# A two-layer hybrid trunk on one core: scale loads, cast order, a table load and layer norm sums rearranged

## What is computed

```python
shift, scale, gate = jnp.split((cond @ w_ada[layer] + b_ada[layer])[:, None, :], 3, axis=-1)
h = rms_norm(x, norm_g[layer]) * (1.0 + scale) + shift
...
u = causal_depthwise_conv(a_half * jax.nn.sigmoid(b_half), conv_b_w[layer]) + conv_b_b[layer]
y_b = jax.nn.silu(layer_norm(u, ln_b_g[layer], ln_b_b[layer])) * jax.nn.silu(z_b)
...
merged = (g_a * (y_a @ w_proj_a[layer]) + g_b * (y_b @ w_proj_b[layer])
          + g_c * (y_c @ w_proj_c[layer]))
x = x + gate * (merged @ w_out[layer])
```

## Time and profile before

| | |
|---|---|
| median of 3 runs | 2340.78 us (2339.74 to 2343.28) |
| the profiled execution's own time | 2340.51 us |
| its span, first to last instruction | 2338.7 us |
| PE / PEld (weight loads) busy | 2255.2 us (96%) / 2040.3 us (87%) |
| POOL busy | 1646.5 us (70%) |
| DVE busy | 1141.1 us (49%) |
| ACT busy | 955.9 us (41%) |
| mean granted TensorE clock | 0.977 of full |
| moved by DMA | 479.65 MB, mean 205 GB/s |

### The profile page before, as it was taken

One profiled execution on the slowest core, in us unless ns is written; L12 is line 12 of the kernel. 1 busy time (PEld: TensorE's weight loads), 2 busy tenths in 40 slices (PEclk: granted clock), 3 DMA queues, 4 the chain that ended last, 5 costly groups with the idle time before them and its releaser, 6 DMA issues.

```text
span 2338.7 us, 40293 instructions
## 1 busy us (share of the span) xinstructions
PE 2255.2 (96%) x16408; PEld 2040.3 (87%) x16408; DVE 1141.1 (49%) x1682; ACT 955.9 (41%) x1037; POOL 1646.5 (70%) x676
## 2 busy tenths in 40 slices
PE   5799999999999999999899999999999999999999
PEld 3789999987779988888899999998777899888899
DVE  5849883854443443443522894665544335421110
ACT  3234444472322544434234344437433244444442
POOL 1468778765554788987666886876655458888876
PEclk8789999999999999999999999999999999999999
DMA  9967545544442589897865664554444337976664
GB/s 370 386 210 225 164 142 177 161 148 124 129 137 92 200 310 332 296 329 284 323 208 181 195 213 142 168 166 145 138 134 134 113 118 279 343 233 190 204 207 154
DMA packets 228840, 479.65 MB, mean 205 GB/s; under 512 B 22080, under 2 KB 26304, under 8 KB 220128
## 3 DMA queue, kind: packets, MB, share of 16 engines
q1 hardware_dynamic: 227392, 475.50, 61.1%
q10 hardware_dynamic: 1312, 2.23, 0.3%
HBM read 471.25 MB, written 6.29 MB: 204 GB/s over the span
## 4 chain that ended last, share of the span: by engine, by line
POOL 48%; issue 35%; PE 16%; POOLq 1%; DVE 0%; ACT 0%; DVEq 0%; ACTq 0%
POOL wl L519 48%; PE ps L908 5%; PE ps L910 5%; PE ps L909 5%; POOLq L518 1%; PE ps L1331 0%; PE ps L997 0%; POOLq L514 0%; DVE xs L1985 0%; DVE ps L1709 0%; ACT gate L528 0%; POOLq L519 0%; DVEq L1367 0%; ACTq L770 0%; DVEq L1708 0%
## 5 line engine op out<-in xcount | busy, mean ns | idle before, releaser
L519 POOL TENSOR_TENSOR wl<-raw,wh 128x1024 fp32r<-128x1024 f32 x672 | 1646.3, 2460 | 679.2 <-ACT wh L540 677.8
L540 ACT CAST wh<-raw 128x1024 fp32r<-128x1024 f32 x672 | 702.8, 1049 | 1227.4 <-PE ps L910 1069.0
L908 PE MATMUL ps<-ah,wh 128*128 128x256 f32 x3008 | 873.8, 290 | 40.8 <-DVE al L1477 21.6
L909 PE MATMUL ps<-al,wh 128*128 128x256 f32 x3008 | 861.0, 286 | 0.0
L910 PE MATMUL ps<-ah,wl 128*128 128x256 f32 x3008 | 860.5, 286 | 0.0
L908 PEld LDWEIGHTS ps<-ah,wh 128*128 128x128 f32 x3008 | 588.0, 195 | 48.1 <-DVE al L1477 21.9
L909 PEld LDWEIGHTS ps<-al,wh 128*128 128x128 f32 x3008 | 587.8, 195 | 4.5 <-issue 4.1
L910 PEld LDWEIGHTS ps<-ah,wl 128*128 128x128 f32 x3008 | 587.4, 195 | 0.0
L908 PE MATMUL ps<-wh,ah 128*128 128x512 f32 (+1 forms) x832 | 325.7, 391 | 0.0
L910 PE MATMUL ps<-wh,al 128*128 128x512 f32 (+1 forms) x832 | 318.7, 383 | 0.0
L909 PE MATMUL ps<-wl,ah 128*128 128x512 f32 (+1 forms) x832 | 318.5, 383 | 0.0
(11 more groups left out here) (259 smaller groups left out, 1810.9 us busy)
## 6 DMA issues: line engine op xcount, KB each, us to landing
raw<-w_in SPq DMA_DIRECT2D x512, 512.0 KB, 3.5
modw<-w_ada SPq DMA_DIRECT2D x64, 1024.0 KB, 7.6
adaw<-w_ada SPq DMA_DIRECT2D x64, 512.0 KB, 9.6
raw<-w_out SPq DMA_DIRECT2D x64, 512.0 KB, 5.0
raw<-w_pc SPq DMA_DIRECT2D x32, 512.0 KB, 3.6
raw<-w_pb SPq DMA_DIRECT2D x32, 512.0 KB, 5.7
raw<-w_pa SPq DMA_DIRECT2D x32, 512.0 KB, 4.9
gbias<-b_gate SPq DMA_DIRECT2D x24, 256.0 KB, 4.3
```

Of the source, the lines that this page charges most:

```text
L519: nc.gpsimd.tensor_tensor(wl[:, s], raw[:, s], wh[:, s].bitcast(F32), ALU.subtract).then_inc(sem("w_split"), 1)
L540: A.copy(wh[:, s], raw[:, s]).then_inc(sem("w_rounded"), 1)
L908: M.matmul(o, lh, rh, start=start, stop=False, skip_group_check=True)
L909: M.matmul(o, lh, rr, start=False, stop=False, skip_group_check=True)
```

## The change

- **Scale loads.** Units 4 to 15 were loaded and used four per output group; now the first group has units 4 and 5, the second 6 to 10, the third 11 to 15. The load of unit 4 comes one round later in SP's list, that of 5 two later, and so on by `SCALE_AT`. Unit 2 of scale moves on DVE ahead of the three `merged_low`, and adds into `acc` instead of PSUM (UNIT_S is 3); unit 3 stays behind the last merge.
- **Casts.** ACT casts five rounds, not two, before it waits for `yb_ready` and copies to `yh`; three follow.
- **Root's table.** An activation Sqrt of one column is put before the squares of the last group of layer 0. Its result goes to `craw`, which nothing reads.
- **Layer norm sums.** DVE first adds the 8 tiles of `ub`, and later of `lnt`, with one `tensor_reduce` each into the new `lss` (128 x 256 each); PE sums over partitions with one matmul each, not eight. The first reduce lies in the third turn of branch c, after the second step of the inverse; the second between `scan_v(2)` and `z_silu(2)`.

```diff
-        UNIT_A, UNIT_W, UNIT_S = 4, 4, 2
+        UNIT_A, UNIT_S = 4, 3
+        UNIT_W = (UNIT_A, 6, 11, KT)
...
-        SCALE_AT = {(0, 3): 4, (0, 5): 5, (0, 6): 6, (0, 7): 7, (1, 1): 8, (1, 3): 9, (1, 5): 10, (1, 7): 11,
-                    (2, 1): 12, (2, 3): 13, (2, 5): 14, (2, 7): 15}
+        SCALE_AT = {(0, 4): 4, (0, 7): 5, (1, 1): 6, (1, 3): 7, (1, 4): 8, (1, 6): 9, (1, 7): 10,
+                    (2, 1): 11, (2, 3): 12, (2, 4): 13, (2, 6): 14, (2, 7): 15}
...
-                rounds(hc + 8, 2)
+                rounds(hc + 8, 5)
                 act.wait_ge(sem("yb_ready"), L1)
                 act.wait_ge(sem("w_used"), proj_end)
                 A.copy(yh[:], ub[:]).then_inc(sem("yh_ready"), 1)
-                rounds(hc + 10, 6, 2)
+                rounds(hc + 13, 3, 1)
...
                     rounds(hc, 3)
+                    A.activation(craw[:, 0:1], epsb[:, 0:1], ACT.Sqrt)
                     for half in range(2):
                         act.wait_ge(sem("x_half"), half + 1)
...
-                    for kt in range(CT):
-                        mm = M.matmul(pb[3][:, 0:T], ones, ub[:, kt], start=kt == 0, stop=kt == CT - 1)
-                    mm.then_inc(sem("ln_sum"), 1)
+                    pe.wait_ge(sem("ln_tiles"), L1)
+                    M.matmul(pb[3][:, 0:T], ones, lss[:, 0], start=True, stop=True).then_inc(sem("ln_sum"), 1)
...
-                    for kt in range(CT):
-                        mm = M.matmul(pb[3][:, T:2 * T], ones, lnt[:, kt], start=kt == 0, stop=kt == CT - 1)
-                    mm.then_inc(sem("ln_var"), 1)
+                    M.matmul(pb[3][:, T:2 * T], ones, lss[:, 1], start=True, stop=True).then_inc(sem("ln_var"), 1)
...
+                def ln_tiles(n):
+
+                    if n == 0:
+                        V.tensor_reduce(lss[:, 0], ub[:].rearrange("p c t -> p t c"), AX.X, ALU.add
+                                        ).then_inc(sem("ln_tiles"), 1)
...
-                    prep_turn(i, split_yc if i == 0 else None)
+                    prep_turn(i, split_yc if i == 0 else ln_tiles if i == 2 else None)
...
-                V.tensor_tensor(lnt[:, 4:8], ub[:, 4:8], ub[:, 4:8], ALU.mult).then_inc(sem("ln_sq"), 1)
+                V.tensor_tensor(lnt[:, 4:8], ub[:, 4:8], ub[:, 4:8], ALU.mult)
                 scan_v(2)
+                V.drain()
+                V.tensor_reduce(lss[:, 1], lnt[:].rearrange("p c t -> p t c"), AX.X, ALU.add
+                                ).then_inc(sem("ln_sq"), 1)
                 z_silu(2, 0, zs[1])
...
+                units(2, 3)
                 for q in range(3):
                     merged_low(q)
                 merge(3, hc, 12 * layer + 8, False)
-                units(2, 4)
+                units(3, 4)
...
-                            for kt in range(UNIT_A + UNIT_W * j, UNIT_A + UNIT_W * (j + 1)):
+                            for kt in range(UNIT_W[j], UNIT_W[j + 1]):
```

More of the change, by code:

```diff
@@ L241, in trunk @@
         lnt = sb("lnt", 122, [CT, T])
+        lss = sb("lss", 172, [2, T])
         xs = sb("xs", 130, [KT, T])
```

## The result

| | before | after |
|---|---|---|
| median | 2340.26 us (2338.14 to 2343.28, 4 runs) | 2315.37 us (2313.75 to 2318.0, 4 runs) |
| ratio | | 0.9894, 95% interval 0.9879 to 0.9909 |
| profiled execution, span | 2340.51, 2338.7 us | 2315.05, 2313.3 us |
| mean granted clock | 0.977 | 0.982 |

The change gains 24.9 us (1.06%); 30.6 us were forecast, 5.7 us too much. The range of 2305 to 2318 us held the time, and the sign was right. A second set of runs gave 2316.99 us and a ratio of 0.9894 (0.9876 to 0.9912).

The account below looks back on a forecast made before the run. PE, busy in 96% of the span, was taken as the bound. Casts 10.2, sums 11.4, scale loads 8.1 and table 0.9 us made 30.6 us, so 2340.8 - 30.6 = 2310.2 us, range 2305 to 2318.

Parts of the forecast that it names:

- I take the whole excess: Second za group, both layers: five casts ahead remove all time lost at PE's two stops, 6.2 + 4.0 = 10.2 us.
- The part of the bound that named POOL as late behind the later cast: Casts' lower bound, second za group: 5 us gained if POOL is still late by half of each stop.
- PE without idle at the second za group: Expected sign in the changed profile: no PE idle there in both layers, with casts of five rounds ahead.
- I left one eighth of 3.27 us: Layer norm sums: seven of eight matmuls go, 2.86 of 3.27 us, twice per layer, 11.4 us in all.
- The rule of the Trainium skill's page "SBUF — State Buffer": Rival for the new reduces: strided reads make them slow; at 9.1 us each, 15.4 us lost, 2326 us, chance 0.06.
- My cover of 4.2 us: First reduce, between two steps of the inverse: PE is held only from about 4.2 us on, one for one.
- I had said 1138 us: Output stage: SP stands before unit 8 until about 1138 us, when DVE has done unit 6.
- late by about 1 us, and single rounds behind a unit by up to 2.6 us: Rounds of the second and third output groups wait on DMA; 2 us given back, bounds 0 and 8.
- DMA becomes the bound: Rival for output groups two and three: three rounds 2.6 us late each, 6 us given back, 2316 us, chance 0.2.
- some 2 us of the range: Lower end of the range: one less stretch at 1.2 GHz somewhere, some 2 us faster.

Follow-up runs that it names:

- the doubled reduce: The changed kernel with the first reduce over tiles done twice, its result used once; measured once, 2328.62 us.
- the other placing: The changed kernel with DVE doing three, five and four scale units in the first three output groups, loads moved to match; 2316.25 us, ratio to before 0.9883.

## Why the prediction was right, and where it was off

The change did what the mechanism said at each of its places, and the time lies inside the range; the forecast was 5.7 us too high. By term:

- **Casts.** Forecast 10.2 us, measured 10.1 at the stops, net 7.7 us. The step that failed is "I take the whole excess": it gave every split 2.46 us, while those of rounds 208 and 211 took 4.4 us in both layers, each beside a DVE instruction with two SBUF inputs. The part of the bound that named POOL as late behind the later cast had the right victim; PE idles 0.24 to 0.66 us there, and a round costs up to 0.95 us more. The sign "PE without idle at the second za group" was wrong by that.
- **Sums.** Forecast 11.4 us, measured 12.1: I left one eighth of 3.27 us, 0.41, and what stays takes 0.25.
- **The reduce.** I took 2.29 us and the price is 3.83 to 3.88, 1.7 times the adjacent one. The rule of the Trainium skill's page "SBUF — State Buffer", section "Specifications (TRN2)", that I had set as a rival (each access that crosses to a new 16-byte line pays a penalty) agrees in direction. But the two reduces differ in their outputs as well, 256 sums of 8 elements against 8 of 256, and no run separates the two. The size lay inside the cover. My cover of 4.2 us was confirmed by the doubled reduce (3.18 us held, 3.3 worked out), so the time was right although the price was not. With 0.4 us to spare that is partly luck.
- **Scale loads.** Forecast 10.1 gone and 2 back. Measured 9.9 gone and 3.55 back. The stop is as foretold: SP stands until DVE has done unit 6, and that came at 1125.46 us. I had said 1138 us on the clock of the kernel before; the casts and sums of layer 0 had taken 12.1 us from all times by then (6.0 and 2 x 3.03), which makes 1125.9. The term "late by about 1 us, and single rounds behind a unit by up to 2.6 us" was sized at 2 us and is 3.55, in five rounds. The DMA share from 1133 to 1176 us is 0.93 at 350 GB/s, less than the 397 of the earlier trace rows; but it is 1.03 from 1140 to 1150 us, where PE waits longest. That the stop for unit 8 is the cause is not shown: the other placing has no such stop and gives 3.16 us back, but it has a stand of 8.1 us before unit 5. The rival "DMA becomes the bound", which I gave 0.2, is the other part of this; at 6 us it was priced too high. Which part is how large stays open.
- **Table.** Forecast 0.9, measured 0.8 (PE idle 6.26 to 5.30 us, a step of 0.55 alone). Alone it cannot be told from no change.
- **What the sum lacked.** The clock appeared only as a gain behind stops that went, and as some 2 us of the range. The trace of before had a half-clock stretch behind three of the four one-column blocks, and I had not looked at what PE did ahead of each.

Together: 30.6 forecast less 2.4 (POOL), 1.5 (scale loads), 0.3 (scale and casts at the stops), 0.1 (table), plus 0.7 (sums) is 27.0; the remaining 2 us to the measured 24.9 are, by the profiles, clock and single waits, and lie within what one kernel's runs differ by.

## What to carry to other kernels

Before moving work beside a co-running engine, list which of its instructions share a port with the neighbour, and price the neighbour's instruction as theirs plus its own: a split of 2.4 us took 4.4. A cover is worth working out even for an operation whose price is unknown, since it told here at which price the time would change. Test a supposed cause by an edit that brings no second one: the other placing of the loads took one stop of SP away and made another, and so could not tell the stop from DMA's rate. And on a kernel that keeps TensorE busy, read the granted clock behind every block of tiny matmuls: spreading 64 of them gained 7 us, nearly a third of what the whole change gained, and took no work away.

## What the runs showed of the hardware

- A DVE `tensor_reduce` of 2048 elements a partition to 256 outputs, reading elements 1 KB apart, took 3.83 to 3.88 us; one over adjacent elements, 2048 to 8 outputs, took 2.29.
- A POOL `tensor_tensor` of 128x1024 took 4.38 to 4.46 us instead of 2.41 beside a DVE instruction with two SBUF inputs, and DVE's own took 3.12 instead of 2.29 us where POOL had started first. Beside a DVE `tensor_scalar` from SBUF to SBUF the split took 3.32 us. Beside a DVE instruction with one input in SBUF and one in PSUM it took 2.41.
- 32 records of one-column matmuls in one block (3.6 to 4.8 us, PE never idle) brought 3.4 to 6.8 us at 1.2 GHz at 32 of 40 places in ten profiles; in pieces of four records, at 0 of 12 in three.
